# Second mixer with its tokens stored by grid columns: each block of 128 queries scores 256 keys in place of 512

## The reference, cut to what matters

```python
def neighbourhood_attention(q, k, v, rpb):
    bsz, s, nh, dh = q.shape
    rows = s // GRID_W                      # 512 // 64 = 8
    kh = min(NA_KH, rows)                   # 8
    kw = NA_KW                              # 16
    ...
    cols = jnp.arange(GRID_W)
    col_start = jnp.clip(cols - kw // 2, 0, GRID_W - kw)
    col_idx = col_start[:, None] + jnp.arange(kw)[None, :]
    dc = col_idx - cols[:, None] + (NA_KW - 1)
    def row_fn(i):
        rs = jnp.clip(i - kh // 2, 0, rows - kh)
        k_win = lax.dynamic_slice_in_dim(kg, rs, kh, axis=1)[:, :, col_idx]
        ...
        sc = jnp.einsum('bjhd,bajkhd->bhjak', q_row, k_win).astype(jnp.float32) * scale
        ...
        sc = (sc + bias[None]).reshape(bsz, nh, GRID_W, kh * kw)
        pr = jax.nn.softmax(sc, axis=-1)...
        return jnp.einsum('bhjak,bajkhd->bjhd', pr, v_win)
```

## Time and profile before

| what | value |
|---|---|
| three timed runs | 3356.19, 3356.84, 3360.86 us |
| median | 3356.84 us |
| span of the profiled execution | 3360.6 us |
| PE busy | 3260.5 us (97%) |
| DVE, ACT, POOL busy | 1552.4, 1082.0, 304.6 us |
| DMA, mean | 134 GB/s |

### The profile page before, as it was taken

The page is one execution under the profiler, slowest core; times in us unless marked ns, Lnnn a source line. Parts: engine busy times, 40 slices in busy tenths (PEclk is TensorE's granted clock), DMA queues, the critical chain, the costliest instruction groups (busy, mean ns, idle before and its releaser), DMA issues. The chain is left out here.

```text
span 3360.6 us, 47546 instructions
## 1 busy us (share of the span) xinstructions
PE 3260.5 (97%) x20620; PEld 2495.8 (74%) x20620; DVE 1552.4 (46%) x2219; ACT 1082.0 (32%) x1586; POOL 304.6 (9%) x356
## 2 busy tenths in 40 slices
PE   9999999999999999999999999988999999989988
PEld 7888887888888888888688888768976888534422
DVE  5443457544436444333754433685458544301112
ACT  4222226432224222223632223563344323200001
POOL 1000131200001000000210000301011300100000
PEclk9999999999999999999999999999999999999999
DMA  3223440122223222332222223301010222899998
GB/s 144 100 89 95 153 133 32 51 98 91 94 95 107 100 100 81 99 134 76 77 88 90 99 90 96 109 32 49 4 55 29 94 94 109 331 427 423 425 427 348
DMA packets 62800, 450.90 MB, mean 134 GB/s; under 512 B 8704, under 2 KB 10368, under 8 KB 32640
## 3 DMA queue, kind: packets, MB, share of 16 engines
q1 hardware_dynamic: 62592, 447.86, 35.6%
HBM read 440.49 MB, written 2.10 MB: 132 GB/s over the span
## 5 line engine op out<-in xcount | busy, mean ns | idle before, releaser
L551 DVE TENSOR_TENSOR w_lo<-slot,w_hi 128x2048 fp32r<-128x2048 f32 (+4 forms) x243 | 487.1, 2005 | 335.0 <-ACT w_hi L542 333.5
L166 PE MATMUL bank<-xa,w_hi 128*128 128x512 f32 x1368 | 535.7, 392 | 3.0 <-DVE w_lo L3096 3.0
L167 PE MATMUL bank<-xa,w_hi 128*128 128x512 f32 x1368 | 532.4, 389 | 0.0
L168 PE MATMUL bank<-xa,w_lo 128*128 128x512 f32 x1368 | 532.3, 389 | 0.0
L542 ACT ACTIVATE w_hi<-slot 128x2048 fp32r<-128x2048 f32 (+4 forms) x243 | 406.0, 1671 | 340.6 <-PE bank L168 331.9
L166 PE MATMUL bank<-xb,w_hi 128*128 128x512 f32 x832 | 324.7, 390 | 0.9 <-DVE w_lo L551 0.8
L167 PE MATMUL bank<-xb,w_hi 128*128 128x512 f32 x832 | 323.7, 389 | 0.0
L168 PE MATMUL bank<-xb,w_lo 128*128 128x512 f32 x832 | 323.7, 389 | 0.0
L166 PEld LDWEIGHTS bank<-xa,w_hi 128*128 128x128 f32 x1368 | 256.8, 188 | 64.5 <-issue 5.4
L168 PEld LDWEIGHTS bank<-xa,w_lo 128*128 128x128 f32 x1368 | 256.8, 188 | 53.6
L167 PEld LDWEIGHTS bank<-xa,w_hi 128*128 128x128 f32 x1368 | 256.8, 188 | 53.5 <-issue 1.2
(11 more groups left out here) (497 smaller groups left out, 4974.6 us busy)
## 6 DMA issues: line engine op xcount, KB each, us to landing
slot<-in_w_gu SPq DMA_DIRECT2D x87, 1024.0 KB, 4.7
slot<-in_exp_gate SPq DMA_DIRECT2D x25, 2048.0 KB, 14.4
slot<-in_exp_up SPq DMA_DIRECT2D x24, 2048.0 KB, 15.1
slot<-in_exp_down SPq DMA_DIRECT2D x24, 2048.0 KB, 15.9
slot<-in_w_dn SPq DMA_DIRECT2D x64, 704.0 KB, 4.0
slot<-in_w_gate SPq DMA_DIRECT2D x24, 768.0 KB, 4.2
xe<-in_exp_up SPq DMA_DIRECT2D x8, 2048.0 KB, 13.5
xe<-in_exp_down SPq DMA_DIRECT2D x8, 2048.0 KB, 15.3
```

The lines of the kernel that those rows point to most:

```text
L166: e.matmul(out, w[0], x[0], start=(j == 0), stop=False)
L167: e.matmul(out, w[0], x[1], start=False, stop=False)
L168: return e.matmul(out, w[1], x[0], start=False, stop=(j == n - 1))
L551: dve.e.tensor_tensor(lo, slot(k, b), hi.bitcast(F32), ALU.subtract).then_inc(L.up("w_lo", b))
```

## The change

The tokens of the second mixer are stored in column order (position = 8 * column + row). A block of 128 queries is then 16 grid columns, and its windows reach from 8 columns ahead of it to 8 behind: 256 keys. Key tiles of 128 are cut at a shift of 64 (`key_tile`): tile i is positions 64+128(i-1) to 64+128i, and tile 0 is the first 64 and the last 64 positions together. Query block i uses tiles (0,1), (1,2), (2,3), (3,0). For blocks 1 and 2 the two tiles lie side by side and one score matmul of 256 columns does both; blocks 0 and 3 ("edge" units, 16 of 32) have two of 128.

- The FFN with index 2 writes xa (hi on ACT, lo on DVE) with a read of h at a stride of 64 elements and a dense write; the root of the norm reads its PSUM bank the same way. The output sum on DVE reads its PSUM bank at a stride of 8 elements and h densely.
- Value tiles follow the key tiles. Tile 0 isn't contiguous, so ACT (`act_edges`) and POOL (`pool_edges`) copy its 128 positions of all eight xa pairs into `xe`, 16 copies of 128x128, and POOL one of 1/rms.
- The four transposes by residue class and their small copy are left out in this mixer.
- Scores, probabilities and their transposes are 256 wide in place of 512, and two v tiles are multiplied in place of four. Bias is 128x768 per head in place of 128x1024.

The diff, cut to its core:

```diff
+def from_rows(x):
+    return x.rearrange("p (r c) -> p c r", c=64)
+def by_cols(x):
+    return x.rearrange("p (c r) -> p c r", r=8)
+def key_tile(x, i):
+    return x[:, 64 + (i - 1) * P:64 + i * P] if i else x.rearrange("p (a t) -> p a t", t=64)[:, 0:8:7, :]
...
-    m.att = AttentionMap(a, 512, 3)
+    m.xe, m.rstd_edge = [a.pair("xe_c", P) for _ in range(KT)], a.buf(P, "rstd_edge")
+    m.att = AttentionMap(a, 256, 3)
...
-        act.e.activation(x[i][0], k.h[i], ACT.Copy, scale=vec(k, gain, i)).then_inc(L.up("x_hi", nm, i))
+        src, dst = (from_rows(k.h[i]), by_cols(x[i][0])) if by_column else (k.h[i], x[i][0])
+        act.e.activation(dst, src, ACT.Copy, scale=vec(k, gain, i)).then_inc(L.up("x_hi", nm, i))
...
+    if by_column:
+        src, hi, lo = from_rows(src), by_cols(hi), by_cols(lo)
+    dve.e.scalar_tensor_tensor(out=lo, in0=src, scalar=vec(k, gain, i), in1=hi, op0=ALU.mult,
                                op1=ALU.subtract).then_inc(L.up("x_lo", nm, i))
...
+    if st == "c":
+        pe.wait_ge(*L.at("rstd_edge"))
...
-        e.tensor_tensor(k.h[m], k.banks.of("out", st, m)[:, :], k.h[m], ALU.add).then_inc(L.up("h", nx, m))
+        out, h = k.banks.of("out", st, m)[:, :], k.h[m]
+        if st == "c":
+            out, h = out.rearrange("p (c r) -> p r c", r=8), h.rearrange("p (r c) -> p r c", c=64)
+        e.tensor_tensor(h, out, h, ALU.add).then_inc(L.up("h", nx, m))
...
+C_KEYS = ((0, 1), (1, 2), (2, 3), (3, 0))
...
+            a, z = C_KEYS[i]
+            edge, place = 0 in C_KEYS[i], (0, 1, 1, 2)[i]
+                scores.append([[(q, key_tile(keys, a)), (q, key_tile(keys, z))] if edge else [(q, keys[:, i * P - 64:i * P + 192])]])
-                              v=[[m.v[:, j, h * 64:h * 64 + 64] for j in range(4)] for h in (2 * t, 2 * t + 1)],
+                              v=[[m.v[:, j, h * 64:h * 64 + 64] for j in (a, z)] for h in (2 * t, 2 * t + 1)],
...
+def act_edges(k, nm):
+    for j in range(KT):
+        act.wait_ge(*L.at("x_lo", nm, j))
+        e.activation(m.xe[j][0].rearrange("p (a t) -> p a t", a=2), key_tile(k.xa[j][0].bitcast(F32), 0), ACT.Copy)...
+def pool_edges(k, nm):
+    pool.wait_ge(*L.at("rstd", nm))
+    e.tensor_copy(m.rstd_edge.rearrange("p (a t) -> p a t", a=2), key_tile(k.rstd, 0)).then_inc(L.up("rstd_edge"))
+    for j in range(KT):
+        pool.wait_ge(*L.at("x_lo", nm, j))
+        e.tensor_copy(m.xe[j][1].rearrange("p (a t) -> p a t", a=2), key_tile(k.xa[j][1].bitcast(F32), 0))...
...
-        pe_values(k, "c", g, b["c_v"] + g, 256, k.xa, tok)
+        pe_values(k, "c", g, b["c_v"] + g, 256, k.xa, key_tile, ("edge_hi", "edge_lo"), k.c.xe)
...
     for j in range(1, 8):
         act_weight(k, b["c_qk"] + j + 1)
+        if j == 2:
+            act_edges(k, nm)
...
     pool_norm(k, "n5")
+    pool_edges(k, "n5")
     pool_attention(k, "c", k.c.att, c_units(k))
```

More of the change, by code:

```diff
@@ L1 @@
+import math
 from contextlib import ExitStack
@@ L272, in plan_memory @@
     m.v = a.buf(4096, "vc").rearrange("p (i c) -> p i c", i=4)
-    m.bias = [a.buf(1024, "bias") for _ in range(4)]
+    m.bias = [a.buf(768, "bias") for _ in range(4)]
     m.rT = a.buf(8, "rT")
-    m.att = AttentionMap(a, 512, 3)
+    m.xe, m.rstd_edge = [a.pair("xe_c", P) for _ in range(KT)], a.buf(P, "rstd_edge")
+    m.att = AttentionMap(a, 256, 3)
     a = after_xb.copy()
@@ L599, in act_root @@
     act.wait_ge(*L.at(*free))
-    act.e.activation(k.rstd, k.banks.of("norm", nm)[:, :], ACT.Sqrt, scale=1.0 / D, bias=k.eps).then_inc(L.up("root", nm))
+    src, dst = k.banks.of("norm", nm)[:, :], k.rstd
+    if by_column:
+        src, dst = from_rows(src), by_cols(dst)
+    act.e.activation(dst, src, ACT.Sqrt, scale=1.0 / D, bias=k.eps).then_inc(L.up("root", nm))
     k.sq_last = ("squares_in", nm)
@@ L780, in pe_rstd_turn @@
     pe.wait_ge(*L.at("rstd", nm))
+    if st == "c":
+        pe.wait_ge(*L.at("rstd_edge"))
     for i in range(4):
-        last = e.transpose(bank[:, i * P:(i + 1) * P], tok(k.rstd, i), k.ident)
+        part = tok(k.rstd, i) if st == "ab" else key_tile(k.rstd, i) if i else k.c.rstd_edge
+        last = e.transpose(bank[:, i * P:(i + 1) * P], part, k.ident)
     last.then_inc(L.up("rstd_turned", st, 0))
+    if st == "c":
+        return
     bank, freed = k.banks.take(("rT", st, 1), ("rT", st, 1))
@@ L792, in dve_rstd_turn, with pe_values @@
     dve, L = k.dve, k.led
-    for z in range(2):
+    for z in range(1 if st == "c" else 2):
         dve.wait_ge(*L.at("rstd_turned", st, z))
         dve.e.tensor_copy(rT[:, 4 * z:4 * z + 4], f4(k.banks.of("rT", st, z)[:, :])[:, :, 0]).then_inc(L.up("rT", st, z))
-def pe_values(k, st, g, b, width, x, sel, ready=()):
+def pe_values(k, st, g, b, width, x, sel, ready=(), edge=None):
     pe, e, L = k.pe, k.pe.e, k.led
@@ L807, in pe_values, with act_values @@
                 pe.wait_ge(*L.at(name, st, j))
-            last = three(e, bank[:, 0:width], each(lambda p: sel(p, i), x[j]), at(w, j), j, KT)
+            lhs = edge[j] if edge and i == 0 else each(lambda p: sel(p, i), x[j])
+            last = three(e, bank[:, 0:width], lhs, at(w, j), j, KT)
         last.then_inc(L.up("v", st, g, i, also=[("w_used", b)] if i == 3 else []))
-def act_values(k, st, g, width, dst, rcol):
+def act_values(k, st, g, width, dst, rcol, turned=1):
     act, e, L = k.act, k.act.e, k.led
@@ L871, in pe_attention @@
                         q, keys = u["scores"][par][z][x]
-                        w = keys.shape[-1]
+                        w = width(keys)
                         last = e.matmul(banks[par][:, off:off + w], q, keys, start=True, stop=True)
@@ L963, in dve_attention @@
                     sc = m.sc[s % len(m.sc)][par]
-                    w = sum(x[1].shape[-1] for x in u["scores"][par][z])
+                    w = sum(width(x[1]) for x in u["scores"][par][z])
                     bank, top = k.banks.of("scores", st, s, par, z), stat[:, 2 * z + par:2 * z + par + 1]
@@ L3362, in _layout @@
     rpb = f["rpb_c"][0]
[L3363 to L3369, removed]
+    t = np.full((16, P, 3, 256), NEG, rpb.dtype)
+    key = np.arange(S)
+    tiles = [np.concatenate([key[0:64], key[448:512]])] + [key[64 + i * P:64 + (i + 1) * P] for i in range(3)]
+    for place, i in enumerate((0, 1, 3)):
+        kt = np.concatenate([tiles[j] for j in C_KEYS[i]])
+        kc, kr = kt // 8, kt % 8
+        for p in range(P):
+            c, r = (i * P + p) // 8, p % 8
+            lo = min(max(0, c - 8), 48)
+            seen = (kc >= lo) & (kc < lo + 16)
+            t[:, p, place, seen] = rpb[:, kr[seen] - r + 7, kc[seen] - c + 15]
+    a["rpb"] = t.reshape(16, P, 768)
     a["w_ple"] = np.stack([np.concatenate([_cols(f["w_ple_gate"][i]), _cols(f["w_ple_proj"][i])], axis=2)
```

36 lines of the change are left out of this document (24 added, 12 removed).

## The result

The changed kernel takes 3316.01 us (median of 4 runs, 3314.88 to 3320.82). The kernel before took 3357.66 beside it (4 runs, 3356.19 to 3360.86). The ratio is 0.9878, with a 95% interval of 0.9864 to 0.9891, and the medians differ by 41.65 us. In two later sets the same pair gave 3320.08 against 3359.26 and 3318.35 against 3357.97, a ratio of 0.9883 (0.9869 to 0.9898) both times. So the kernel is faster by 39 to 42 us, set by set. Forecast were 3317 us and a gain of 40.4.

A forecast was written before the change was run, and what follows sets the result against it. PE, busy 97% of the span, was taken to pace the attention; 40.0 us saved there plus 0.4 from transposes took the median 3356.84 to 3316.4, called 3317. Range 3311 to 3328, with rivals A and B included.

The forecast's parts named there:

- interior step: Second mixer's attention: each of 27 steps takes 2.03 us on PE against 3.32, with 256-wide pieces.
- edge units: Sixteen of 32 attention units score two tiles of 128: +0.05 us each, +0.8 in all, ends 0 and +9.8.
- filling: Start of the second mixer's attention, before the steps: 5.35 us (ends 5.0 and 6.1) against 8.03.
- draining: End of the second mixer's attention, after the steps: 5.9 us (ends 5.8 and 7.0) against 9.13.
- residue-class transposes: The four transposes left out in the second mixer: 0.40 us saved on PE.
- strided reads: Ahead of the mixer: last tile's ACT and DVE passes grow 0.44 to 1.23 us, under 1.29 spare; cost 0.
- Rival B: Attention: handshakes pace the step at 2.36 us, not PE; +8.9 us, 3326 in all; chance 0.09.
- rival A: Attention: the edge units' weight loads set their pace, +0.61 us for each of 16; 3326 in all; chance 0.10.
- Copies for tile 0: Eight on ACT, nine on POOL, needed by PE some 50 us later: cost 0, or 5 us without cover.
- Rival C: Attention: bias transfers come late; if two take 10 us, +12 us, 3329 in all; chance 0.03.
- Rival D: Attention: granted clock falls because PE has shorter bursts with gaps; slower, 3384 at the 1.2 GHz level; chance 0.02.
- Rival E: A stage behind, the DMA-fed experts' part at the end, gives half the gain back: 3337; chance 0.03.

The follow-up runs named there:

- Experiments three and four: Kernel after with one key tile of 128 per unit (three): 3297.96 us, ratio 0.9823; with three tiles, 384 keys (four): 3338.62 us, ratio 0.9946.
- experiment two: Kernel after with a unit's queries read as every fourth token in place of 128 dense ones: 3325.73 us, ratio 0.9908.

## Why the prediction was right

The terms of the sum, as forecast and as the trace of the kernel after has them:

| term | forecast | trace |
|---|---|---|
| interior step, 27 steps | 2.03 each | 2.03 each |
| edge units, all | +0.8 | under +0.2 |
| filling | 5.35 | 5.17 |
| draining | 5.9 | 5.73 |
| attention | 66.9 | 65.73 |
| saved in the attention | 40.0 | 41.2 |
| residue-class transposes | 0.40 | 0.48 |
| value products | 0 | 0.22 |
| strided reads, copies, bias | 0 | 0 |
| sum | 40.4 | 41.9 (medians 41.65, 39.18, 39.62) |

The mechanism was the one forecast. The closeness of the number, 3317 for 3316.01, is in part luck: by the trace the sum was 1.5 us short, and the medians of the kernel after move by 4 us from set to set, while its attention takes 65.73 or 65.74 us in every profile of it.

- **The step.** It was read from the earlier trace rows, where the same code ran units of the same shape; piece by piece the new step has the same durations. Experiments three and four show that it holds because PE paces, and not by luck of two equal bounds. DVE came out at 1.73 per step against 1.86 forecast: its biased maximum took 422 ns, less than the 477 of the first mixer's. ACT came out at 1.63, under the 1.90 that I took as its bound. Rival B's 2.36 was no bound of handshakes but PE's own pace at 2.5 tiles.
- **The edge units.** The value was near the right end. The reason, that the loads of the earlier trace rows are strided, was only argued then; experiment two shows it. That kernel's 3325.73 falls on rival A's 3326 by luck of two terms: A had +0.61 for each edge unit and nothing for the interior ones, and the strided loads gave +0.50 and +0.13.
- **Filling, draining** were each too long by under 0.2 us. With the edge units (0.8 forecast, some 0.02 by the 27 steps) they make up 1.1 of the 1.2 us by which the attention came out shorter than forecast; rounding is the rest.
- **Strided reads.** ACT's pass took 1.21 against 1.15 forecast. DVE's pass did not grow at all, 1.17 against 1.27 in the earlier trace rows, so of the feared 0.44 to 1.23 only 0.40 came, and of the cover of 1.29 there is 0.89 left.
- **Copies for tile 0** ended by 1470.5 on ACT and 1457 on POOL, more than 60 us before PE reads them at 1532.35.
- **Bias.** The widest time to landing was 6.6 us against the 8.1 that a buffer has, and DVE waits for no transfer in the attention. Rival C did not occur.
- **Rival D** did not occur: the clock is 1.00 in the whole stage. **Rival E** neither: the distance of 42.6 us stays from the end of the attention to the scan at 2225, and is not given back by the end.

What waits there are in the attention show how little is left, the kernel after, 1580 to 1645 (total, times, longest):

```profile
POOL xa L953 <- DVE att L977: 162.3, 31, 128.4
ACT den_inv L921 <- PE bank L878: 10.1, 30, 0.7
PEld bank L890 <- ACT scores L941: 6.5, 31, 1.2
...
PEld bank L874 <- DVE probsT L986: 4.3, 13, 0.3
```

The weight loads of the transposes wait 6.5 us in all for ACT's exponentials, 0.2 per step, but PE streams the piece before them meanwhile. That it costs nothing is seen from the step, which lies on the line of experiments three and four, and at one tile such waits are gone altogether.

## What to carry to other kernels

Where one engine paces a pipeline with no gaps, the price of a smaller step is best read from a place in the same trace that runs the same code at the smaller shape, and then each other engine's busy time per step is held against it. That engine's own time at the larger shape also explains a mean that looks like a limit of handshakes (2.36 here). A bound taken from a row with another access pattern (strided for dense) may be far off, and the nearest row is the one with the same pattern, even if it does other work. Two single executions can differ by 4 us here in a stage that the change doesn't touch: follow the distance between equal instructions through both traces before giving a stage credit for it.

## What the hardware showed that I had not expected

- A stride in the stationary operand (64 partitions, 128 columns, every fourth token, fp32) makes a load 326 ns where a dense one is 186, and a group of eight with its products 1.14 us where it was 0.64. A group of four with products of 256 columns hides most of it: 0.77 for 0.64.
- A step of the tokens by 256 bytes costs ACT 0.50 us on a 128x512 read from SBUF (0.71 to 1.21), and DVE nothing (1.27 dense, 1.17 strided). ACT's root and DVE's sum into h, which read PSUM with a stride, took 0.69 each, no more than a dense pass.
- The 11 products ahead of the scan change nothing that can be measured (3316.5 without them), although the clock is at its lower level when they begin. The scan itself took between 174.2 and 178.8 us in the profiled executions of these kernels, with the same code, and by and large was the longer, the lower its granted clock (1.00 to 0.78 in its first 30 us).
